# A different division of the opening between TensorE, VectorE and the DMA queues in a fused two-block transformer kernel

## The reference

```python
cs = jax.nn.silu(c)
mod = cs @ mod_w[l] + mod_b[l]
sh_m, sc_m, g_m = mod[:, :D], mod[:, D:2 * D], mod[:, 2 * D:3 * D]
h = modulate(rmsnorm(x, norm_mix[l]), sh_m, sc_m)   # rmsnorm(x) * (1 + scale) + shift
mix = rglru_mixer(h, lru_w_in[l], ...)              # h @ w_in, causal conv, gates, scan, w_out
...
s_own = s_own + bias_tab[:, t5_bucket(dist_own)]    # later: attention's relative bias, by distance
```

## Time and profile before

| what | value |
|---|---|
| median of 3 runs | 1810.8 us (1806.93 to 1814.6) |
| the profiled execution's own time | 1805.07 us |
| its span | 1803.4 us |
| granted TensorE clock, mean | 0.976 |
| DMA over the span | 353.80 MB, 196 GB/s |

### The profile page before, as it was taken

The page is one execution under the profiler, slowest core; times in us unless marked ns, Lnnn a source line. Parts: engine busy times, 40 slices in busy tenths (PEclk is TensorE's granted clock), DMA queues, the critical chain, the costliest instruction groups (busy, mean ns, idle before and its releaser), DMA issues.

```text
span 1803.4 us, 30032 instructions
## 1 busy us (share of the span) xinstructions
PE 1713.6 (95%) x11890; PEld 1595.1 (88%) x11890; DVE 1180.2 (65%) x1492; ACT 897.7 (50%) x1238; POOL 109.2 (6%) x161
## 2 busy tenths in 40 slices
PE   7988999999999999999999999988999998999996
PEld 4987999998899989999898899978999898899986
DVE  7988889867774456555675655565655675665556
ACT  4576533466543445343575543455433567543445
POOL 2110211100010000000020000000000003000000
PEclk9998999999999999999998999998999999999998
DMA  9983799946465554555441455534555442355550
GB/s 382 333 318 140 272 381 362 361 148 246 158 217 189 185 189 147 188 185 186 143 173 44 163 194 195 185 130 140 201 184 187 174 143 92 112 204 186 178 194 36
DMA packets 61924, 353.80 MB, mean 196 GB/s; under 512 B 6522, under 2 KB 9738, under 8 KB 27792
## 3 DMA queue, kind: packets, MB, share of 16 engines
q1 hardware_dynamic: 40064, 281.24, 42.6%
q0 software_dynamic: 18384, 66.66, 10.1%
q10 hardware_dynamic: 3392, 4.72, 0.8%
HBM read 349.45 MB, written 3.15 MB: 196 GB/s over the span
## 4 chain that ended last, share of the span: by engine, by line
PE 81%; DVE 9%; ACT 5%; issue 3%; DMA 2%; POOL 1%; DVEq 0%; ACTq 0%; POOLq 0%
PE bank L499 24%; PE bank L500 24%; PE bank L501 24%; DVE w_lo L1540 2%; ACT w_hi L1019 2%; PE bank L531 1%; PE bank L533 1%; PE bank L532 1%; PE bank L674 1%; DVE shared L2109 1%; DVE shared L1562 1%; DMA shared<-in_mods 1%; DVE x L2118 1%; DVE work L1924 1%; PE bank L557 1%
## 5 line engine op out<-in xcount | busy, mean ns | idle before, releaser
L499 PE MATMUL bank<-a_hi,w_hi 128*128 128x256 f32 x2648 | 757.2, 286 | 13.5 <-DVE a_lo L1613 3.8
L501 PE MATMUL bank<-a_hi,w_lo 128*128 128x256 f32 x2648 | 753.4, 285 | 0.0
L500 PE MATMUL bank<-a_lo,w_hi 128*128 128x256 f32 x2648 | 753.3, 284 | 0.0
L499 PEld LDWEIGHTS bank<-a_hi,w_hi 128*128 128x128 f32 x2648 | 512.4, 194 | 19.9 <-issue 10.4
L500 PEld LDWEIGHTS bank<-a_lo,w_hi 128*128 128x128 f32 x2648 | 512.4, 194 | 2.7 <-issue 0.5
L501 PEld LDWEIGHTS bank<-a_hi,w_lo 128*128 128x128 f32 x2648 | 512.0, 193 | 0.0
L1807 DVE TENSOR_TENSOR w_lo<-raw,w_hi 128x2048 fp32r<-128x2048 f32 x144 | 330.1, 2292 | 246.2 <-ACT w_hi L1160 246.2
L1160 ACT CAST w_hi<-raw 128x2048 fp32r<-128x2048 f32 x144 | 274.0, 1904 | 270.2 <-PE bank L501 270.2
L1540 DVE TENSOR_TENSOR w_lo<-raw,w_hi 128x2048 fp32r<-128x2048 f32 x122 | 279.5, 2294 | 135.9 <-ACT w_hi L1019 135.7
L1019 ACT CAST w_hi<-raw 128x2048 fp32r<-128x2048 f32 x122 | 231.6, 1907 | 90.8 <-PE bank L501 84.1
L499 PE MATMUL bank<-w_hi,hid_hi 128*128 128x512 f32 x548 | 216.2, 395 | 3.9 <-DVE hid_lo L2283 3.1
(11 more groups left out here) (251 smaller groups left out, 1904.3 us busy)
## 6 DMA issues: line engine op xcount, KB each, us to landing
raw<-in_stream SPq DMA_DIRECT2D x266, 1024.0 KB, 4.8
shared<-in_mods POOLq DMA_DIRECT2D x104, 512.0 KB, 6.8
grow<-in_rows POOLq DMA_DIRECT2D x12, 512.0 KB, 4.0
work<-in_mods POOLq DMA_DIRECT2D x8, 512.0 KB, 9.6
bias_rows<-work ACTq DMA_DIRECT2D x1, 2048.0 KB, 23.2
x<-in_x_t SPq DMA_DIRECT2D x1, 1024.0 KB, 6.0
x<-in_x_d ACTq DMA_DIRECT2D x1, 1024.0 KB, 7.6
work<-bias_rows ACTq DMA_DIRECT2D x1, 1024.0 KB, 8.6
```

The costliest lines, as they stand in the source:

```text
L499: pe.matmul(out, w_h, v_h, start=start, stop=False, skip_group_check=True)
L500: pe.matmul(out, w_h, v_l, start=False, stop=False, skip_group_check=True)
L501: return pe.matmul(out, w_l, v_h, start=False, stop=stop, skip_group_check=True)
```

## The change

The opening is divided anew. In the words of the diff:

- TensorE takes half 0 of each chunk of the first group. Eight products per chunk have 128 x 128 of the half as weights and one column, `cs[:, kc]`, as the moving operand. They add up in eight columns of bank 2. `mod_taken` counts chunks. VectorE keeps half 1 and counts each one twice, and the sums over partitions are eight instead of 16. VectorE adds the shift's bias columns itself (`sums_joined`).
- GpSimd waits for `mod_taken` ahead of the even halves and for `mod_step` ahead of the odd ones. The second group's halves wait for `mod_step` of 16.
- SyncE asks for slab 0 at `mod_step` 4, slab 1 at 6 and slab 2 at 14.
- The eight bias-row products become one (33 x 8 by 33 x 512). ScalarE copies its 8 x 512 result, stores it to a small DRAM tensor, and later issues a DRAM-to-DRAM transfer that repeats each row 128 times.
- VectorE starts with the first group. Root, and the low parts of slabs 0 and 1, stand inside that loop. The `lam` chain stands behind the low part of slab 2.
- ScalarE makes the high part of slab 2 behind the normed input and both transfers.
- `ones` is the first memory fill, and 14 unused products stand first on TensorE. The later unused products are 4 instead of 17.

```diff
+    row_store = nc.dram_tensor("bias_row_store", (HEADS, 512), F32, kind="Internal").ap()
-            sp.wait_ge(mod_step, 9)
             for s in range(RING):
+                sp.wait_ge(mod_step, (4, 6, 14)[s])
                 sp.dma_start(raw[:, s, :], stream[s]).then_inc(landed[s], 16)
@@ GpSimd
+            nc.gpsimd.memset(ones[:, :], 1.0).then_inc(ones_ready, 1)
-                pool.wait_ge(mod_step, u - 2 * MOD_RING + 1)
+                if u % 2 == 0:
+                    pool.wait_ge(mod_taken, (u - 2 * MOD_RING) // 2 + 1)
+                if u % 2 or u >= 4 * MOD_RING:
+                    pool.wait_ge(mod_step, u - 2 * MOD_RING + 1 if u < 4 * MOD_RING else 4 * MOD_RING)
@@ TensorE
+            pe.wait_ge(ones_ready, 1)
+            for _ in range(14):
+                pe.matmul(bank[1][:, 0:P], ones[:, :], ones[:, :], start=True, stop=True)
+            pe.wait_ge(mask_row_set, 1)
+            pe.wait_ge(s_rb, 16)
+            pe.wait_ge(s_oh, 16)
+            pe.matmul(bank[0][0:HEADS, :], rb_sb[:, :], onehot_sb[0:33, :], start=True, stop=True).then_inc(row_mm, 1)
+            norm_stat(N_MIX0)
+            pe.wait_ge(cs_ready, 1)
             pe.wait_ge(const_ready, 1)
-            for h in range(HEADS):
-                if h >= 2:
-                    pe.wait_ge(row_ev, h - 1)
-                pe.matmul(bank[h % 2][:, :], rbb[0:33, h, :], onehot_sb[0:33, :], start=True, stop=True).then_inc(row_mm, 1)
-            norm_stat(N_MIX0)
-            pe.wait_ge(row_ev, HEADS)
-            pe.wait_ge(mod_step, 14)
-            keep_warm(8)
-            mod_reduce(G_MIX0, 7)
+            for kc in range(8):
+                slot, landings = mod_slot(2 * kc)
+                pe.wait_ge(mod_landed[slot], 16 * landings)
+                for m in range(8):
+                    mm = pe.matmul(bank[2][:, m:m + 1], mod_slots[slot][:, m * P:(m + 1) * P], cs[:, kc:kc + 1],
+                                   start=(kc == 0 and m == 0), stop=(kc == 7), skip_group_check=True)
+                mm.then_inc(mod_taken, 1)
+            mod_reduce(G_MIX0, 7, range(8, 16))
+            pe.wait_ge(row_ev, 1)
+            keep_warm(4)
             need_slab(B_WIN)
-            keep_warm(9)
@@ ScalarE
-            for h in range(HEADS):
-                act.wait_ge(row_mm, h + 1)
-                act.copy(bias_rows[:, h, :], bank[h % 2][:, :]).then_inc(row_ev, 1)
+            act.wait_ge(row_mm, 1)
+            act.copy(bias_rows[0:HEADS, :], bank[0][0:HEADS, :]).then_inc(row_ev, 1)
+            act.wait_ge(row_ev, 1)
+            act.dma_start(row_store, bias_rows[0:HEADS, :]).then_inc(s_row_store, 16)
             rsqrt(N_MIX0, D)
-            split_to(RING)
+            split_to(2)
             normed_hi(A_MIX0, a_out, lambda c: modcol(G_MIX0, c))
             act.dma_start(x[:, :, :], x_d.rearrange("(t p) d -> p t d", p=P)).then_inc(x_landed, 16)
-            act.wait_ge(row_ev, HEADS)
-            act.dma_start(scratch.rearrange("h p s -> p h s"), bias_rows).then_inc(s_rows, 16)
+            act.wait_ge(s_row_store, 16)
+            act.dma_start(scratch, row_store.unsqueeze(1).to_broadcast([HEADS, P, 512])).then_inc(s_rows, 16)
+            split_to(RING)
@@ VectorE
-            dve.wait_ge(s_rb, 16)
-            dve.tensor_copy(rbb[0:32, :, :], rb_sb[:, :].unsqueeze(2).to_broadcast([32, HEADS, P])).then_inc(rbb_ready, 1)
-            dve.memset(rbb[32:33, :, :], 1.0).then_inc(rbb_ready, 1)
+            dve.memset(rb_sb[32:33, :], 1.0).then_inc(mask_row_set, 1)
+            dve.wait_ge(cs_ready, 1)
+            for kc in range(8):
+                steps[0] += 1
+                mod_half(counts=2)
+                if kc == 3:
+                    root(N_MIX0, D)
+                if kc >= 5 and kc < 7:
+                    split_to(kc - 4)
+            dve.wait_ge(mod_taken, 8)
+            at = COL_AT["mod_b"]
+            dve.tensor_tensor(modc[:, 0:8], bank[2][:, 0:8], cols[:, at:at + 8], ALU.add).then_inc(sums_joined, 1)
+            mod_columns(G_MIX0, 7, 8, 16)
+            scale_of(0, G_MIX0, CH, COL_AT["norm_mix"])
+            dve.wait_ge(scale_ready, 1)
+            dve.wait_ge(sums_joined, 1)
+            normed(A_MIX0, N_MIX0, x_src, lambda c: scale1[:, c:c + 1], a_h, a_l, lambda c: modcol(G_MIX0, c))
+            split_to(RING)
             dve.wait_ge(lam_act, 2)
...
-            dve.wait_ge(cs_ready, 1)
-            for kc in range(8):
-                mod(G_MIX0, kc)
-            root(N_MIX0, D)
-            split_to(1)
-            mod_columns(G_MIX0, 7)
-            scale_of(0, G_MIX0, CH, COL_AT["norm_mix"])
-            split_to(2)
-            dve.wait_ge(scale_ready, 1)
-            normed(A_MIX0, N_MIX0, x_src, lambda c: scale1[:, c:c + 1], a_h, a_l, lambda c: modcol(G_MIX0, c))
-            split_to(RING)
             mod_half(4)
```

More of the change, by code:

```diff
@@ L228, in build @@
         mod_fourth = area(8448, 2048)
-        rbb = area(5120, HEADS, P)
-        bias_rows = area(6144, HEADS, 512)
+        bias_rows = area(6144, 512)
         onehot_sb = area(10240, 512)
@@ L278, in build @@
         warm = sb("warm", [P, 1])
-        rb_sb = sb("rb_sb", [32, HEADS])
+        rb_sb = sb("rb_sb", [33, HEADS])
         def col(name, k):
@@ L290, in build @@
         s_late = sem("late_landed")
-        s_rows = sem("bias_rows_stored")
+        s_row_store, s_rows = sem("bias_row_stored"), sem("bias_rows_stored")
         s_bias = sem("bias_landed")
@@ L311, in build @@
         ident0 = sem("ident_zeroed")
-        rbb_ready = sem("rbb_ready")
+        mask_row_set, ones_ready = sem("mask_row_set"), sem("ones_ready")
+        mod_taken, sums_joined = sem("mod_taken_by_tensor"), sem("shift_columns_made")
         row_mm, row_ev = sem("bias_row_made"), sem("bias_row_copied")
@@ L414, in mod_half @@
                 return mods[u // 2][:, u % 2 * MOD_HALF:(u % 2 + 1) * MOD_HALF]
-            pool.dma_start(rb_sb[:, :], rb_t).then_inc(s_rb, 16)
+            nc.gpsimd.memset(ones[:, :], 1.0).then_inc(ones_ready, 1)
+            pool.dma_start(rb_sb[0:32, :], rb_t).then_inc(s_rb, 16)
             pool.dma_start(onehot_sb[0:33, :], onehot).then_inc(s_oh, 16)
@@ L423, in _ @@
             nc.gpsimd.affine_select(out=ident[:, :], in_=ident[:, :], compare_op=ALU.not_equal, fill=1.0, base=0,
-                                    pattern=[[-1, P]], channel_multiplier=1)
-            nc.gpsimd.memset(ones[:, :], 1.0).then_inc(const_ready, 1)
+                                    pattern=[[-1, P]], channel_multiplier=1).then_inc(const_ready, 1)
             for u in range(2 * MOD_RING, 5 * MOD_RING):
                 slot, _ = mod_slot(u)
-                pool.wait_ge(mod_step, u - 2 * MOD_RING + 1)
+                if u % 2 == 0:
+                    pool.wait_ge(mod_taken, (u - 2 * MOD_RING) // 2 + 1)
+                if u % 2 or u >= 4 * MOD_RING:
+                    pool.wait_ge(mod_step, u - 2 * MOD_RING + 1 if u < 4 * MOD_RING else 4 * MOD_RING)
                 pool.dma_start(mod_slots[slot], mod_half(u)).then_inc(mod_landed[slot], 16)
@@ L716, in attention @@
                         score(k + 3)
-            pe.wait_ge(const_ready, 1)
-            pe.wait_ge(rbb_ready, 2)
-            pe.wait_ge(s_oh, 16)
-            for h in range(HEADS):
-                if h >= 2:
-                    pe.wait_ge(row_ev, h - 1)
-                pe.matmul(bank[h % 2][:, :], rbb[0:33, h, :], onehot_sb[0:33, :], start=True, stop=True).then_inc(row_mm, 1)
-            norm_stat(N_MIX0)
-            pe.wait_ge(row_ev, HEADS)
-            pe.wait_ge(mod_step, 14)
-            keep_warm(8)
-            mod_reduce(G_MIX0, 7)
+            pe.wait_ge(ones_ready, 1)
[7 more added lines that the diff above has]
+            pe.wait_ge(cs_ready, 1)
+            pe.wait_ge(const_ready, 1)
+            for kc in range(8):
[8 more added lines that the diff above has]
+            keep_warm(4)
             need_slab(B_WIN)
-            keep_warm(9)
             need_slab(B_WIN + 1)
@@ L1544, in _, with mod_half @@
             steps = [0]
-            def mod_half(n=1):
+            def mod_half(n=1, counts=1):
                 for _ in range(n):
@@ L1563, in mod_half @@
                                                        op0=ALU.mult, op1=ALU.add)
-                    ins.then_inc(mod_step, 1)
+                    ins.then_inc(mod_step, counts)
                     steps[0] += 1
```

## The result

The changed kernel takes 1814.63 us (median of 18 runs, 1811.24 to 1820.58) against 1809.36 for the kernel before (18 runs, 1802.31 to 1815.24). The ratio is 1.0034, with a 95% interval of 1.0021 to 1.0046: slower by 5.3 us in the medians, and less than 0.5%. The forecast was +1.7 us, no change that can be told, 1802 to 1821. So the time came out on the side forecast and inside the range, with three times the size. (The forecast's 1812.5 started from the 1810.8 of three runs, which lies 1.4 above the median that 18 runs give.) The profiled execution of the changed kernel has a span of 1813.0, 9.6 above the 1803.4 of the one before. That one's own time, 1805.07, lies 4.3 us under its kernel's median, so I read the 9.6 for where the time goes and the 5.3 for how much it is.

The account below looks back on a forecast made before the run. DMA was taken to bound the opening up to the first product, then VectorE, with TensorE's slabs as long; 2.8 us of lateness against the first product's gain (40.0 against 41.06) gave +1.7, so 1812.5 us from 1810.8, range 1802 to 1821.

Parts of the forecast that it names:

- T + 16.9: Opening, VectorE: the first convolution can start 16.9 us after the first slab product T, against the T + 14.1 it needed before.
- TensorE through at 35.0: Opening, TensorE: 128 one-column records at 0.18 us take 23.0 us from about 12, ending 0.7 behind VectorE.
- the landings: Opening, DMA: 11.74 MB must land, by 32.0 us; last half taken at about 33.0, before 31.75; earlier slab requests cost nothing.
- the 40.0 forecast: Opening, TensorE: first product of a slab at 40.0 us against 41.06, or 38.2 at the quick end.
- Rival 4: Opening, DMA: SyncE's early slab requests starve the halves, last half 2 us later, 1814.5 us; chance 0.07.
- Rival 1: VectorE's later waits for halves, 90 to 108 us, absorb part of the lateness: 1806.2 to 1809.7 us; chance 0.22.
- Rival 2: Broadcast with outermost dimension 8 uses few DMA engines; slabs lose up to 5.1 us between 46 and 92: 1817.6; chance 0.17.
- Rival 3: TensorE's one-column records don't overlap, 0.33 us each: +20.8 us, 1831.6; chance 0.06 for above 0.24 us per record.

## Why the prediction was right, and where its sizes were off

The direction rested on one statement: gains at the first product are eaten by what was moved behind it. The second half of it held. **T + 16.9** for the first convolution was measured at 61.44 - 44.52 = 16.92, the late high part, chain and halves included, and the run with the chain first gives back the 2.8 us of lateness (14.10). The chain has 17 operations and not 15; its 3.5 us are read from the rows and stand. The first half failed: there was no gain to eat. The forecast was 1.1 us gained and 2.8 lost. In the two profiles 3.5 are lost up to the first product, 2.8 from there to the convolution and 2.8 behind it. So the direction is earned by the middle term alone. That the time is inside the range is owed to the range's width, and to medians that show only 5.3 of the 9.6 us.

The term that failed is **TensorE through at 35.0**. It was 38.9. The 128 records at 0.18 gave 23.0 us, and TensorE did work 23.0 us on them: 27.1 from 11.84 to 38.92, less two waits of 1.94 and 2.13 for its halves. But that sum is right by luck. The first records took 0.113 us and the last 0.218, and the two kinds happen to average 0.18. The 0.18 came from a count of 11 records in a window of 2 us. The windows of the changed kernel count 11 as well where the spacing is over 0.21, since a record that reaches into the window counts too. What the sum lacked is the 4.1 us of waits: the chunks were never laid against the landings, and behind the second wait three chunks were left to do at the slow rate. The sums took 3.4 instead of 2.9. Columns at 42.42 and 2.1 more give the 44.52, 4.5 later than the 40.0 forecast.

The second term is **the landings**. 11.74 MB at 32.0 was right as traffic (the engines run dry at 32), but a half is usable about 2 us later (34.48 with the low parts out of the way), and the low parts in the loop put it at 36.65. TensorE hid this error. The early slab requests were priced at nothing, on the ground that the same bytes are waited for either way. The bytes are the same, but halves and slabs share the engines, and a half that lands beside slabs took 3.77 us instead of 1.28. The changed kernel asks for its first slab at 14.54, and VectorE then waits 5.89 and 1.80 us for the halves that it takes at 26.76 and 29.85. In the kernel before, early slabs alone cost 2.1 us at the first product. Rival 4 was the nearest to this mechanism; a last half later by 2 us and more was real, as the run with the low parts behind the loop shows (34.48 against 31.75), and TensorE's lateness hid it.

The third is a term that was left out: **what is lost behind the first convolution**, 2.8 us from 55 to 118. Rival 1 expected those waits to absorb lateness. They didn't. The cause stays open. The stretch takes 55.0 and 54.4 us in the two runs with the wide operand, 54.7 in the one with fills and in the kernel before, and 55.9 to 58.9 in all the others. Three of those others are the kernel before with one thing moved (57.3, 56.5, 55.9), and the run with fills has thin records, so thin records alone don't make it.

Rival 2 is out: the wide broadcast moves no mark by more than 0.8 us and the time not at all. Rival 3's price per record (0.33) was never seen; only the slow half of the records, at 0.218, passed its deciding point of 0.18.

What stays open: the profiles differ by 9.6 us and the medians by 5.3. Part of it is that the profiled execution of before was quick for its kernel. Whether its opening was also quicker than usual, one profile can't say. Because of this the marks of single runs, above all where they differ by under 1 us, shouldn't be added up to the us.

## What to carry to other kernels

TensorE at one column per record can read as fully busy while its clock falls, and what it does next then takes nearly double. Where such a product must be made, a moving operand of repeated columns cost next to nothing per record here and kept the clock up, though not through an idle time of 4.45 us in one run. And transfers that are outstanding together share the engines, whatever the order in which they were asked for. Before moving one "earlier", ask which transfer is the last that the critical engine waits for, and how many like it are still outstanding at that moment: the harmless-looking chain of 17 small operations had been the delay that held three slabs back until most halves were in.

## What the runs showed that I hadn't expected

- One moving column or 128: 0.113 and 0.117 us per float32 record at the upper level. At the lower, 0.218 for one column and 0.21 for the sums' 128 columns (16 records from 38.78 to the columns at 42.42, less the 0.2 of the handover).
- The norm's sums are 16 records in both kernels, and the granted clock reads 1.00 for both. They take 6.19 us behind the thin row products in the kernel before and 3.72 behind full products in the changed one. So a 1.00 early in a trace need not mean the upper level; the records' own times decide.
- Three full products behind each chunk of eight thin ones left the clock at 0.50 from 20 us to 52, behind the end of the share.
- Moving 3.5 us of small VectorE operations from ahead of the halves to behind them, in a kernel where VectorE then waits for landings anyway, made its first product 5.2 us later (46.27 against 41.06): 3.7 by the last half, 1.5 by TensorE's slower sums behind its longer idle time.
